# Latent attention on one Trainium2 core: query and key up-projections multiplied together first

## The reference

```python
qm = (rms_norm(mq, mq_norm_g) @ mq_up).reshape(B, L, 4, 128 + 64)
ckv = rms_norm(mkv, mkv_norm_g)                  # rank 128
qm_nope, qm_pe = qm[..., :128], qm[..., 128:]
kv = (ckv @ kv_up).reshape(B, L, 4, 128 + 128)
k_nope, vals = kv[..., :128], kv[..., 128:]
s = (qm_nope @ k_nope.T + rope(qm_pe) @ rope(kpe).T) * 192 ** -0.5
o = softmax(s) @ vals
```

## Time and profile before

| | |
|---|---|
| median of 3 runs | 964.92 us (963.84 to 966.18) |
| profiled execution | 964.14 us, of which the span is 962.3 us |
| mean granted TensorE clock | 0.989 |
| PE busy | 935.7 us (97% of the span), 5349 matmuls and transposes |
| DVE busy | 598.7 us (62%) |
| ACT busy | 312.1 us (32%) |
| POOL busy | 86.5 us (9%) |
| transfers | 83.31 MB, 87 GB/s on average |

### The profile page before, as it was taken

How to read it: one execution, slowest core, us unless ns; L and a number is a source line. 1 busy time by engine, 2 the same in 40 slices (tenths; PEclk the granted TensorE clock), 3 DMA queues, 4 the chain that set the end, 5 groups by cost and what they waited for, 6 DMA issues and landing times.

```text
span 962.3 us, 13792 instructions
## 1 busy us (share of the span) xinstructions
PE 935.7 (97%) x5349; PEld 682.4 (71%) x5349; DVE 598.7 (62%) x1296; ACT 312.1 (32%) x856; POOL 86.5 (9%) x126
## 2 busy tenths in 40 slices
PE   6999999999999999889999999999999999999997
PEld 2447667454567756758998888888989755555886
DVE  3756655996978878895695333431767566653324
ACT  3153110211024666533302234032410575454111
POOL 6010000000000022100213103000000100200001
PEclk9999999999999999899999999999999999999999
DMA  8951541120131401212278006621401110000102
GB/s 252 353 178 59 180 128 47 41 76 13 44 94 47 131 0 45 67 45 68 81 243 290 2 1 176 198 78 45 131 32 57 60 44 1 1 1 1 44 1 110
DMA packets 74578, 83.31 MB, mean 87 GB/s; under 512 B 7013, under 2 KB 68528, under 8 KB 74257
## 3 DMA queue, kind: packets, MB, share of 16 engines
q1 hardware_dynamic: 68706, 69.50, 23.2%
q0 software_dynamic: 2688, 9.53, 3.0%
q10 hardware_dynamic: 3119, 3.39, 1.1%
HBM read 78.85 MB, written 3.56 MB: 86 GB/s over the span
## 4 chain that ended last, share of the span: by engine, by line
PE 92%; DVE 3%; ACT 2%; DMA 1%; SPq 1%; issue 1%; POOLq 0%; POOL 0%; DVEq 0%; ACTq 0%
PE ps L1497 79%; PE ps L1718 5%; PE ps L1516 3%; DMA wring<-in_mod_w 1%; PE ps L1916 1%; PE ps L2125 1%; ACT phase L1411 1%; PE ps L1876 1%; PE ps L1582 1%; PE ps L1626 0%; DVE wring L2702 0%; ACT phase L1414 0%; PE ps L1526 0%; PE ps L1901 0%; DVE phase L2710 0%
## 5 line engine op out<-in xcount | busy, mean ns | idle before, releaser
L1497 PE MATMUL ps<-phase 128*128 128x128 f32 (+4 forms) x880 | 238.1, 420 | 3.1 <-ACT phase L1143 1.9
L1497 PE MATMUL ps<-hT,wring 128*128 128x128 f32 (+3 forms) x848 | 213.4, 409 | 0.1
L1497 PEld LDWEIGHTS ps<-phase 128*128 128x128 f32 (+1 forms) x880 | 151.8, 191 | 77.6 <-issue 50.8
L1497 PEld LDWEIGHTS ps<-hT,wring 128*128 128x128 f32 x848 | 131.8, 192 | 77.6 <-issue 67.7
L1497 PE MATMUL ps<-wring,mix 128*128 128x256 f32 x464 | 101.7, 379 | 1.0 <-issue 1.0
L1497 PEld LDWEIGHTS ps<-wring,mix 128*128 128x128 f32 x464 | 87.8, 190 | 13.4 <-issue 1.6
L1497 PE MATMUL ps<-phase,hT 128*128 128x256 f32 (+3 forms) x336 | 78.8, 391 | 0.1
L1497 PEld LDWEIGHTS ps<-phase,hT 128*128 128x128 f32 x336 | 60.4, 190 | 15.8 <-issue 10.7
L2952 DVE TENSOR_TENSOR phase<-ps,phase 128x512 f32<-128x512 f32 (+1 forms) x33 | 19.3, 591 | 67.9 <-PE ps L1497 65.4
L1718 PE MATMUL ps<-ident,phase 128*128 128x128 f32 x400 | 51.4, 281 | 1.9 <-ACT phase L1414 1.2
L1718 PEld LDWEIGHTS ps<-ident,phase 128*128 128x128 f32 x400 | 47.1, 146 | 8.0 <-issue 4.2
(11 more groups left out here) (428 smaller groups left out, 1264.7 us busy)
## 6 DMA issues: line engine op xcount, KB each, us to landing
wring<-in_mod_w SPq DMA_DIRECT2D x18, 1024.0 KB, 5.4
wring<-in_even_in_w SPq DMA_DIRECT2D x16, 1024.0 KB, 5.9
phase<-in_mod_w SPq DMA_DIRECT2D x6, 1024.0 KB, 5.1
wring<-in_odd_in_w SPq DMA_DIRECT2D x5, 1024.0 KB, 8.4
phase<-in_odd_in_w SPq DMA_DIRECT2D x4, 1024.0 KB, 10.6
wring<-in_odd_out_w SPq DMA_DIRECT2D x4, 1024.0 KB, 4.9
wring<-in_even_out_w SPq DMA_DIRECT2D x3, 1024.0 KB, 11.0
xreg<-decay_rows ACTq DMA_DIRECT2D x5, 512.0 KB, 4.9
```

Source lines behind the costliest of these rows:

```text
L1497: return nc.tensor.matmul(o, l, r, start=first, stop=last)
```

## The change

The score of a latent head is (q_up_h^T m) . (k_up_h^T c) with m the query latent (256) and c the key latent (128). The kernel after multiplies q_up_h by k_up_h^T first and takes the scores straight against c.

- Three new fills `tr_w` ahead of `tr_att`: 12 transposes of 128 x 128 turn q_up (two row halves) and the key part of kv_up; ACT copies them to `qwT` and `kwT`.
- Two new fills `absorb` behind `q_pe`: 8 matmuls of 128 columns give `qkw`; ACT copies them. PE waits for both copies before `q_nope`.
- `q_nope` uses `qkw` in place of `qw`; its sizes stay. The latent scores read `ckvT` in place of `knT`; their sizes stay.
- `k_nope` (8 matmuls, 6 fills, 6 ACT copies) is gone.
- `v_up` moves from behind `scores(1)` to between `scores(0)` and `scores(1)`. DVE's order becomes maxima 0, the six value copies, normalise 0, maxima 1, normalise 1.
- `gb_l[1]` lies elsewhere in SBUF, and its transfer waits for the last `tr_qpe` fill.

```diff
-         ("st2", 8), ..., ("st5", 8), ("tr_att", 3 * NT + 1),
-         ("q_pe", NT), ("q_nope", 5), ("score0", 5), ("k_nope", 6), ("score1", 5), ("v_up", NT + 1), ("tr_qpe", NT),
+         ("st2", 8), ..., ("st5", 8), ("tr_w", 3), ("tr_att", 3 * NT + 1),
+         ("q_pe", NT), ("absorb", 2), ("q_nope", 5), ("score0", 5), ("v_up", NT + 1), ("score1", 5), ("tr_qpe", NT),
...
-            wait_full(pool, start["v_up"] + NT)
+            wait_full(pool, start["tr_qpe"] + NT - 1)
...
+            for n, dst in enumerate((qwT[:, 0, :, :], qwT[:, 1, :, :], kwT)):
+                f = start["tr_w"] + n
+                wait_full(act, f)
+                nc.scalar.activation(dst, bank(f).rearrange("p (h c) -> p h c", h=H), ACT.Copy).then_inc(free(f), 1)
...
             take_gate_columns(5)
+            for k in range(2):
+                f = start["absorb"] + k
+                wait_full(act, f)
+                nc.scalar.activation(qkw[:, k, :, :], bank(f).rearrange("p (h c) -> p h c", h=H), ACT.Copy).then_inc(free(f), 1)
...
             exponentials(0)
-            for h in range(H):
-                f = start["k_nope"] + h
-                wait_full(act, f)
-                nc.scalar.activation(knT[:, h, 0:LS], bank(f), ACT.Copy).then_inc(free(f), 1)
...
             exponentials(1)
...
+            pe.wait_ge(odd_in, 160)
+            for n, weights in enumerate((qw[:, 0, :, :], qw[:, 1, :, :], kw)):
+                turn4(start["tr_w"] + n, lambda h: weights[:, h, 0:P])
...
-                    mm(o, qnT[:, h - 4, toks(t)], knT[:, h - 4, keys], True, False)
+                    mm(o, qnT[:, h - 4, toks(t)], ckvT[:, keys], True, False)
...
+            for n in range(3):
+                wait_drained(pe, start["tr_w"] + n)
+            for k in range(2):
+                f = start["absorb"] + k
+                wait_free(pe, f)
+                for h in range(H):
+                    ins = mm(bank(f)[:, h * P:h * P + P], qwT[:, k, h, :], kwT[:, h, :])
+                ins.then_inc(full(f), 1)
+            for k in range(2):
+                wait_drained(pe, start["absorb"] + k)
...
-                    ins = mm(bank(f), qw[:, k, h, 0:P], mqT[:, k, 0:LS], k == 0, k == 1)
+                    ins = mm(bank(f), qkw[:, k, h, :], mqT[:, k, 0:LS], k == 0, k == 1)
...
             scores(0)
-            for h in range(H):
-                f = start["k_nope"] + h
-                wait_free(pe, f)
-                mm(bank(f), kw[:, h, 0:P], ckvT[:, 0:LS]).then_inc(full(f), 1)
-            for g in range(2):
-                ...
-                    ins = mm(bank(f)[:, h * WC:h * WC + WC], kw[:, 2 * g + h, 0:P], ckvT[:, LS:TOK + P])
-                ins.then_inc(full(f), 1)
-            scores(1)
             for t in range(NT + 1):
                 f = start["v_up"] + t
                 wait_free(pe, f)
                 mm(bank(f), ckvT[:, toks(t)], kw[:, :, P:2 * P]).then_inc(full(f), 1)
+            scores(1)
...
             maxima(0)
-            normalise(0)
-            maxima(1)
             for t in range(NT + 1):
                 f = start["v_up"] + t
                 wait_full(dve, f)
                 nc.vector.tensor_copy(vm[:, t, :], bank(f)).then_inc(free(f), 1)
+            normalise(0)
+            maxima(1)
             normalise(1)
```

More of the change, by code:

```diff
@@ L107 @@
          ("st1", 8), col(LAST[2]), row(LAST[3]), ("in_tm5", NT), col(LAST[3]),
-         ("st2", 8), ("st3", 8), ("st4", 8), ("st5", 8), ("tr_att", 3 * NT + 1),
-         ("q_pe", NT), ("q_nope", 5), ("score0", 5), ("k_nope", 6), ("score1", 5), ("v_up", NT + 1), ("tr_qpe", NT),
+         ("st2", 8), ("st3", 8), ("st4", 8), ("st5", 8), ("tr_w", 3), ("tr_att", 3 * NT + 1),
+         ("q_pe", NT), ("absorb", 2), ("q_nope", 5), ("score0", 5), ("v_up", NT + 1), ("score1", 5), ("tr_qpe", NT),
          ("att", 8 * 11 + 2 * 3 - 1 - 10),
@@ L370, in program @@
         y_l = [view(7680, NT, D), view(0, NT, D)]
-        gb_l = [view(12800, 2, D), view(17152, 2, D)]
+        gb_l = [view(12800, 2, D), view(24832, 2, D)]
         xn = view(23040, NT, D)
@@ L383, in program @@
         qflat = view(24320, NT * WC)
-        qpe, knT = view(24320, NT, WC), view(25600, H, TOK + P)
+        qpe = view(24320, NT, WC)
+        qwT, kwT, qkw = view(25600, 2, H, P), view(26624, H, P), view(27136, 2, H, P)
         vm, kpT = hflat[:, 0:3072].rearrange("p (t n) -> p t n", t=NT + 1), hflat[:, 3072:3072 + TOK + P]
@@ L2099, in _ @@
                 seven_products(s)
+            qw = q_up.rearrange("p k (h c) -> p k h c", h=H)
+            kw = kv_up.rearrange("p (h c) -> p h c", h=H)
+            pe.wait_ge(odd_in, 160)
+            for n, weights in enumerate((qw[:, 0, :, :], qw[:, 1, :, :], kw)):
+                turn4(start["tr_w"] + n, lambda h: weights[:, h, 0:P])
             for t in range(NT + 1):
@@ L2111, in _ @@
                 else:
-                    pe.wait_ge(odd_in, 160)
                     wait_free(pe, f)
@@ L2146, in scores @@
                                 wait_free(pe, f + 1 + g)
-                                mm(bank(f + 1 + g), qnT[:, h0 - 4, toks(g)], knT[:, h0 - 4, 0:LS], True, False)
+                                mm(bank(f + 1 + g), qnT[:, h0 - 4, toks(g)], ckvT[:, 0:LS], True, False)
                             for g in pair:
@@ L2154, in scores @@
                     ins.then_inc(full(f), 1)
-            qw = q_up.rearrange("p k (h c) -> p k h c", h=H)
-            kw = kv_up.rearrange("p (h c) -> p h c", h=H)
             for t in range(NT):
@@ L2174, in _ @@
                 for k in range(2):
-                    ins = mm(bank(f)[:, h * P:h * P + P], qw[:, k, h, 0:P], mqT[:, k, LS:TOK], k == 0, k == 1)
+                    ins = mm(bank(f)[:, h * P:h * P + P], qkw[:, k, h, :], mqT[:, k, LS:TOK], k == 0, k == 1)
             ins.then_inc(full(f), 1)
```

## The result

The changed kernel takes 969.62 us (median of 6 runs, 967.4 to 970.55), the kernel before in the same group 964.84 (963.84 to 966.18): 1.0045 times as long, 95% interval 1.003 to 1.006. It is slower by 0.3 to 0.45%. The forecast was 968.0 in 965.6 to 970.2, slower with a chance of 0.73.

A forecast was written before the change was run, and what follows sets the result against it. It took PE, 92% of the chain, as the bound. Terms 1.0 + 1.8 + 1.0 - 2.1 = +1.7, plus 1.4 for the clock, gave 964.9 + 3.1 = 968.0 us; own range 966.8 to 969.2, 8-in-10 range 965.6 to 970.2.

The forecast's parts named there:

- What bounds it, and the prices from load spacing: Whole chain: 92% PE; a record costs 0.429 us at 512 columns, 0.211 at 256, 0.112 at 128, a transpose 0.109.
- `tr_w`, net +1.0: Ahead of tr_att: 12 transposes add 1.31 us, a 0.32 us wait for DVE's query copy goes; net +1.0.
- `absorb` +1.8 and the wait behind it +1.0: Behind q_pe: 8 matmuls of 128 columns cost 1.8 us, then PE waits 1.0 for ACT's copy ahead of q_nope.
- `k_nope` -5.1; the wait behind `scores(0)` unchanged: Dropping the key products saves 5.1 us; v_up takes their place, so the 0.43 us wait behind scores(0) stays.
- Where the stall goes: Fourth tr_qpe fill: PE waits 3.5 us for exponentials(1), late through DVE's queue; 5.1 + 0.43 removed, loop starts 2.1 earlier.
- Sum ahead of the clock +1.7: Touched stretch: 1.0 + 1.8 + 1.0 - 2.1 = +1.7 us, with bounds +1.2 to +2.5.
- rival A: At the tr_qpe stall: it comes but the clock stays up; +1.7 us, 966.6 (966.1 to 967.4), chance 0.23.
- The clock +1.4: Behind the 3.5 us stall: the clock runs at half level for 3.4 us, costing PE 1.4 us.
- rival B: Behind the tr_qpe stall: the clock is down twice as long; 969.7 us, chance 0.17 together with rival D.
- rival D: Behind absorb: the 1.0 us wait also lowers the clock, +1.7 on the forecast, 969.7 us; chance 0.17 with rival B.
- Forecast +3.1: Whole kernel: 1.7 + 1.4 = +3.1 us on 964.9 gives 968.0 us, chance 0.50.
- Rival C: At tr_qpe: the new stall is absent, so the kernel gets faster by 1.7 us to 963.2, chance 0.10.

The follow-up runs named there:

- e_absorbfirst: The changed kernel with the absorb fills ahead of q_pe, on PE, in ACT's order and in the list of fills: 969.04 us, 1.004 of the kernel before.
- e_cover: The changed kernel with scores 0 ahead of q_nope and v_up behind scores 1, on PE, ACT and DVE: 962.12 us, 0.9965 of the kernel before.
- e_dveorder: The changed kernel with DVE's maxima 1 ahead of normalise 0: 965.50 us, 1.000 of the kernel before.
- e_trfirst: The changed kernel with tr_qpe ahead of scores 1 on PE, ACT and in the fills, DVE's order kept: 965.43 us, 0.9999 of the kernel before.
- e_busy: The changed kernel with four extra, unused 512-column matmuls ahead of the fourth tr_qpe fill: 967.75 us, 1.0019 of the kernel before.

## Why the prediction was right, step by step

- *What bounds it, and the prices from load spacing:* right. The stretch is 5 us of matmuls lighter in `k_nope` and heavier by `tr_w` and `absorb` as counted. The load at the end of `q_nope` that came at 766.95 before came at 771.56, less the 0.85 of the later start 3.76 later, where the forecast had `scores(0)` 3.8 later.
- *`tr_w`, net +1.0:* `q_pe` began 7.20 us after the first transpose, 66 x 0.109. The old wait for DVE went. Right, and the measured 0.109 a transpose held; the estimate from the factor that the Trainium skill gives (TensorE: Matmul & The Clock Gate, Terms) would have been 0.65 too low.
- *`absorb` +1.8 and the wait behind it +1.0:* `q_nope` starts at 764.62, its load, released by ACT, at 764.59. The wait is 0.98 by e_absorbfirst. Right. SiLU (762.42 to 763.47) and the first copy (from 763.37) did queue, and it made next to no difference: the second copy started at 763.9, about when PE ended `absorb`.
- *`k_nope` -5.1; the wait behind `scores(0)` unchanged:* that load stood 1.00 us, as in the kernel before. The size of the term is held by e_cover, 2.79 us shorter where the terms say 2.83. Right.
- *Where the stall goes:* the prediction said the fourth `tr_qpe` fill, with 5.1 + 0.43 us gained and 3.5 given back. The long wait sits there, 3.29 us in the view and 3.5 counted from the end of twelve transposes. e_dveorder and e_trfirst show both causes: take DVE's order away and it shrinks to 1.53; move the fill and the stall follows its bank. Right.
- *Sum ahead of the clock +1.7:* 1.72 in e_busy, 1.63 without the overhang of its extra work. Right. The bounds beside it do not follow: those given with the terms add up to +1.5 to +2.2, not to +1.2 to +2.5. Only rival A's bounds hung on it.
- *The clock +1.4:* in the traces of the changed kernel 1.3 to 1.6 (46.41 to 46.69 less 45.08), or 1.4 to 1.7 counted from the restart. The fall came in all five traces with the 3.3 us wait. That it would come was the better bet, not a certainty: the wait of 3.0 us that the prediction read as harmless (line 1557) was followed by half clock in other traces of the same opening stage. Rival A (the clock stays up) and rival B (twice as long) did not occur; rival D neither, behind the 0.7 us wait the clock stayed at 1.00 (748 to 786 us).
- *Forecast +3.1:* 3.05 to 3.33 in four traces. What parts the run times from the forecast's 968.0 is not in the stretch. The first group's medians were 4.8 apart, the second's 3.5. The step that was short is the base: I added 0.8 us from the profiled execution to the median of three runs (964.9), and the larger groups put the kernel before at 965.5 and 965.8. Its first trace, with the clock at 0.94 in the first 30 us, began the stretch early. With 965.5 to 965.8 as base the forecast's +3.1 gives 968.6 to 968.9 against 969.35 and 969.62 measured (the 969.62 beside a base of 964.84, so there 1.7 us stay open, within the noise of six runs against six).
- *The number, then, was partly luck.* 969.62 lies outside the forecast's own range (966.8 to 969.2) and inside the wider one only because that made room for B and D, whose 969.7 it meets almost exactly. By run time alone B or D would have looked right; only the traces show 3.4 us at half clock and not twice that.
- *Rival C (the stall is not there, 963.2)* did not occur. Its sum holds (e_dveorder, with 1.68 us of stall, comes out even), but even with maxima 1 waiting for nothing but PE that stall was still there. e_cover is faster, by 2.8 and not 1.7, and by another order of PE's work.

## What to carry to other kernels

When an engine that bounds the kernel is handed less work, ask which latency the removed work was covering. Here 5.1 us of key products stood between two softmaxes, and their removal uncovered the chain maxima, exponentials, bank release: 1.68 us of it with maxima 1 in its best place (e_dveorder), 3.45 once `normalise(0)` stood ahead of it too. Count banks in the new order, since the wait moves to whichever fill shares a bank with the one that is freed last, and put the reductions that release another engine ahead of work that nobody asks for yet. Look at the granted clock behind an idle stretch of TensorE of some 3 us, and in more than one execution: here 3.3 us cost their length and about half as much again (1.4 to 1.7 us) each time, while 3.0 to 3.2 us in the opening stage brought the clock down in three traces of five. An order that leaves no such gap turned +3 into -2.8 us with the same arithmetic.

## What the runs showed of the hardware that was not expected

Filling a 3.3 us wait with four useless matmuls made the kernel 1.3 to 1.6 us faster (stretch 45.08 against 46.41 to 46.69). In the first trace of the changed kernel the half clock ended while PE had done nothing but transposes since its restart (792.35 to 796.83). Waits of 1.53 us in the same place and of 1.43 us a bank round later left the clock at 1.00, while one of 1.9 us elsewhere was followed by 0.66. Two executions can part at a wait of equal length: behind 3.02 us the clock was 1.00, behind 3.07 us at the same place 0.50. And the same program on the same inputs differs by 3 us between executions, nearly all of it ahead of its 750th us (behind the stretch every trace of the changed kernel takes 169.3 to 169.4 us), which decides whether a change of 1 us can be seen in run times at all.
